# Operands of one decoder layer placed at multiples of 512 bytes in SBUF

## The reference, cut to what matters

```
h = rms_norm(x, ln1_g);  proj = h @ w_in                 # input projection
o = concat(gated_deltanet(proj...), sparse_attention(proj...))
x = x + o @ w_out                                        # output projection
h = rms_norm(x, ln2_g);  q = h @ w_query                 # 8 heads, two halves of 128
# per token and head: 16 best keys of 128 in each half, 16 best pairs -> gates, experts
act = gelu(h . u[expert]);  x = x + sum(gate * act * v[expert])   # 16384 experts
out = rms_norm(x, final_g)
```

## Time and profile before

| | |
|---|---|
| median of three runs | 1706.88 us |
| the profiled execution's own time | 1708.15 us |
| its span, first to last instruction | 1706.2 us |
| mean granted clock of TensorE, share of 2.4 GHz | 0.979 |
| TensorE busy with matmuls | 1630.3 us, 96% |
| VectorE, ScalarE, GpSimd busy | 78%, 40%, 32% |
| HBM traffic | 404 MB, 237 GB/s over the span |

### The profile page before, as it was taken

One profiled execution on the slowest core, in us unless ns is written; L12 is line 12 of the kernel. 1 busy time (PEld: TensorE's weight loads), 2 busy tenths in 40 slices (PEclk: granted clock), 3 DMA queues, 4 the chain that ended last, 5 costly groups with the idle time before them and its releaser, 6 DMA issues.

```text
span 1706.2 us, 26801 instructions
## 1 busy us (share of the span) xinstructions
PE 1630.3 (96%) x9303; PEld 1387.8 (81%) x9303; DVE 1333.9 (78%) x2453; ACT 682.1 (40%) x1070; POOL 540.2 (32%) x383
## 2 busy tenths in 40 slices
PE   7998888968999999999999999999999999999998
PEld 5876675545777999999999999998888788888886
DVE  6744568777642689999999999858888888888887
ACT  5574323154422343433354444433333333333334
POOL 2000000014420467888732334313333333322220
PEclk9999998879999999999999999999999999999999
DMA  4320010001223468888889999999999999999995
GB/s 140 99 95 27 2 39 1 25 25 50 87 86 125 143 196 289 282 286 280 262 295 359 336 348 342 340 335 401 371 372 376 368 372 367 379 353 334 350 354 191
DMA packets 148992, 404.47 MB, mean 237 GB/s; under 512 B 14084, under 2 KB 71684, under 8 KB 145448
## 3 DMA queue, kind: packets, MB, share of 16 engines
q1 hardware_dynamic: 108584, 243.92, 42.3%
q0 software_dynamic: 36864, 134.23, 20.7%
q10 hardware_dynamic: 3456, 25.17, 3.7%
HBM read 350.83 MB, written 52.44 MB: 236 GB/s over the span
## 4 chain that ended last, share of the span: by engine, by line
PE 54%; DVE 10%; DMA 1%; issue 1%; ACT 1%; POOL 0%; DVEq 0%; SPq 0%; ACTq 0%
PE bank L1555 10%; PE bank L1556 10%; PE bank L1557 10%; PE bank L2073 7%; PE bank L2077 7%; PE bank L2074 7%; DVE own_waste L1858 3%; PE bank L2097 3%; DMA front<-active_scratch 1%; DVE back L1909 1%; DVE rt_num L1880 1%; DVE rt_num L1873 1%; DVE rt_work L1874 1%; DVE rt_pos L1902 0%; DVE rt_pos L1899 0%
## 5 line engine op out<-in xcount | busy, mean ns | idle before, releaser
L2073 PE MATMUL bank<-hi_parts,rt_u_parts 128*128 128x384 f32 x1024 | 351.3, 343 | 0.0
L2074 PE MATMUL bank<-lo_parts,rt_u_parts 128*128 128x384 f32 x1024 | 344.1, 336 | 0.0
L1555 PE MATMUL bank<-rt_u_parts,rt_w_hi 128*128 128x512 f32 x768 | 304.1, 396 | 1.1 <-DVE rt_w_lo L1471 1.1
L1557 PE MATMUL bank<-rt_u_parts,rt_w_hi 128*128 128x512 f32 x768 | 303.7, 395 | 0.0
L1556 PE MATMUL bank<-rt_u_parts,rt_w_lo 128*128 128x512 f32 x768 | 303.7, 395 | 0.0
L1415 ACT ACTIVATE rt_u_parts<-raw 128x1024 fp32r<-128x1024 f32 x128 | 135.8, 1061 | 337.1 <-PE bank L1557 326.7
L1773 ACT ACTIVATE rt_u_parts<-raw 128x1024 fp32r<-128x1024 f32 x126 | 133.8, 1062 | 337.3 <-PE bank L2077 299.3
L2132 POOL DMA_INDIRECT qy<-v_dram,own_experts x128 | 133.3, 1041 | 361.0 <-DVE qy L1489 355.0
L2126 POOL DMA_INDIRECT h<-u_rows_dram,own_experts x128 | 172.7, 1349 | 236.4 <-DVE own_waste L1858 222.4
L1471 DVE TENSOR_TENSOR rt_u_parts<-raw,rt_u_parts 128x1024 fp32r<-128x1024 f32 x128 | 156.7, 1224 | 83.0 <-ACT rt_u_parts L1415 77.7
L1820 POOL TENSOR_TENSOR rt_u_parts<-raw,rt_u_parts 128x1024 fp32r<-128x1024 f32 x66 | 162.8, 2467 | 129.5 <-ACT rt_u_parts L1773 128.0
(11 more groups left out here) (356 smaller groups left out, 2602.8 us busy)
## 6 DMA issues: line engine op xcount, KB each, us to landing
raw<-u_dram SPq DMA_DIRECT2D x128, 512.0 KB
raw<-v_dram SPq DMA_DIRECT2D x128, 512.0 KB
active_scratch<-rt_act SPq DMA_DIRECT2D x128, 192.0 KB
gates_scratch<-front ACTq DMA_DIRECT2D x12, 1024.0 KB
gates_scratch<-back ACTq DMA_DIRECT2D x12, 1024.0 KB, 7.9
front<-gates_scratch SPq DMA_DIRECT2D x8, 1536.0 KB
front<-active_scratch SPq DMA_DIRECT2D x64, 192.0 KB
back<-active_scratch SPq DMA_DIRECT2D x64, 192.0 KB
```

Of the source, the lines that this page charges most:

```text
L1555: mm(bank, w_hi[:, j, block], v_hi[:, j, cols], start=False, stop=False)
L1557: last = mm(bank, w_hi[:, j, block], v_lo[:, j, cols], start=False, stop=stop)
L2073: mm(bank, u_hi[:, j % 2, chunk[c]], hi[:, c, 0:TD], start=c == 0, stop=False)
L2074: mm(bank, u_hi[:, j % 2, chunk[c]], lo[:, c, 0:TD], start=False, stop=False)
```

## The change: offsets, and no instruction

Three paddings and one move of a declaration. `aligned` allots an unused tensor that fills up to the next multiple of 512. It is called ahead of `x_stream` and ahead of `conv`. `w`, `w_hi` and `w_lo` are declared first in the route stage instead of last but one. Each engine's instructions are the same, in the same order.

```diff
+LINE = 512
...
@@ route_stage
+        w, w_hi, w_lo = sb("w", [P, 2, TD]), sb("w_hi", [P, 2, TD], F32R), sb("w_lo", [P, 2, TD], F32R)
         act_s = sb("act", [P, 4, TD])
...
         iota, row_of = sb("iota", [P, PTOP], BF16), sb("row_of", [P, P], F16)
-        w, w_hi, w_lo = sb("w", [P, 2, TD]), sb("w_hi", [P, 2, TD], F32R), sb("w_lo", [P, 2, TD], F32R)
...
@@ build
+        def aligned(ctx, name, unit):
+
+            short = -nc.sbuf_base % unit
+            if short:
+                ctx.enter_context(nc.sbuf_tensor(name, [P, short // 4], F32))
+
+        aligned(outer, "stream_place", LINE)
         x = outer.enter_context(nc.sbuf_tensor("x_stream", [P, DC, T], F32))
...
+            aligned(inner, "conv_place", LINE)
             conv, conv_parts = twins(inner, "conv", QKV_T)
```

## The result

The changed kernel took 1688.46 us, the median of four runs (1684.09 to 1689.56), against 1708.87 us for the kernel before (four runs, 1706.8 to 1710.9). The ratio is 0.9876, with a 95% interval from 0.9852 to 0.99. The forecast was 1688 us.

What follows compares the result with a forecast made beforehand. It took TensorE's distance between matmul starts as the bound. Value stage 15.2, minus 1 for a stall, plus tail 4.3 gave 18.5 us off 1708.15: 1689.7 profiled, 1688 at the median, range 1678 to 1709.

Steps and rivals of the forecast that it cites:

- What bounds: Value stage and tail run at TensorE's pace; with the matmul count unchanged, only the distance between starts could shrink.
- The value stage, 15.2 us: Moving w_hi and w_lo from 416 to 0 takes 2304 matmuls from 233.3 to 226.7 ns each, saving 15.2 us.
- the one stall: Value stage before: VectorE waited 3.2 us for activations behind a load of gates, of which 1.1 reached TensorE.
- a further stall: Value stage: 1 us taken off the gain for one more place where transfers come late.
- The transfers rival: Value stage: gate loads stall TensorE more, losing some 9 us of the 15, so 1697 us; chance 0.08.
- The tail, 4.3 us: Moving conv from 480 to 0 takes 7.5 ns off each of the tail's 576 matmuls, 4.3 us.
- Everything else, 0: Input and route stages, operands going from 128 to 0, were taken to keep their distances: 0 us.
- the rival of a whole line: All stages: the 13.3 ns surplus comes from operands beginning inside a 512-byte unit; 71 us less, 1636; chance 0.07.
- The cause: Float32r matmuls: weights starting off a multiple of 64 (or 128) cost about 7 ns more per matmul.
- The rival of the slower side: Value stage: equal remainders make accesses meet, adding 5 ns on 2304 matmuls, +11.5 us, so 1718; chance 0.06.
- The rows on plain float32: Mixer stage: L1159 at 592 ns and L386 at 591 were read as not feeling the start; 0, bound 1 us.

Runs made afterwards that it cites:

- w_alone: Kernel before with only w, w_hi and w_lo moved, from remainder 416 to 128 (by 512); ratio 0.9897.
- conv_alone: Kernel before with only conv moved, from remainder 480 to 0, hi and lo staying at 128; ratio 0.9993.
- by32: Changed kernel with rt_u_parts, conv and w at remainder 32, hi, lo and qy left at 0; 1696.12 us, one run.
- moving32: Changed kernel with hi, lo, raw, front, qy and rt_u_parts at remainder 32, conv and w left at 0; 1705.20 us, one run.
- mapC: Changed kernel with rt_u_parts at remainder 128, conv at 448 and w at 320; 1698.73 us, one run.
- conv128: Kernel before with only conv moved, from remainder 480 to 128, w staying at 416; ratio 0.9981.
- both128: Kernel before with conv and w at remainder 128 and nothing else moved; ratio 0.9891, median 1688.99 us.
- mapA: Changed kernel with conv at remainder 256 and w at 128, all that moves at 0; 1704.37 us, one run.
- mapB: Changed kernel with conv at remainder 64 and w at 256, all that moves at 0; 1688.77 us, one run.
- w16: Changed kernel with w_hi and w_lo starting 16 bytes behind a multiple of 512, conv at 96; 1706.33 us, one run.
- cols_apart: Changed kernel with route matmuls at 512 columns, value stage at 384, rt_u_parts at 32, conv at 320, w at 0; 1829.10 us, one run.
- cols_equal: Changed kernel with route matmuls at 512 columns, value stage at 384, rt_u_parts, hi, lo and w at 0, conv at 192; 1806.21 us, one run.

## Why the prediction was right in time and wrong in cause

*What bounds.* Right. TensorE's distances were 19.5 of the 24.0 us between the two profiles, and nothing else was late next.

*The value stage, 15.2 us.* Right: the distance fell by the 6.6 ns that were taken, to a tenth of a nanosecond. w_alone shows it by itself, 0.0103 of 1709, 17.6 us, of which 1.5 may be the one stall. The 1 us that I took off for a further stall had the wrong sign: no stall came, and the one of before went as well (16.8 us by the profile). The transfers rival is refuted by 383 GB/s without a wait.

*The tail, 4.3 us.* Right for the change, 4.2 in the profile. As a term of its own it would have been wrong: I priced `conv` from 480 to 0, which alone gives (234.3 − 232.8) × 576 = 0.9 us. It comes only because `hi` and `lo` go to 0 as well, which the prediction did not count as needed. That the change did both is luck for this term.

*Everything else, 0.* Right. The input stage stayed at 389 ns and the route stage at 173.3, so the rival of a whole line is out: with all at 0, the 13.3 ns are there as before.

*The cause.* This step failed: "All three are multiples of 32. Only 128 is a multiple of 64 or of 128." From stages that all have the moving operand at 128, I took the difference between 128 and 416 or 480 for a property of the weights' own start. The same rows allow another reading, that weights at 128 are good since what moves is at 128. The moving operand had one remainder in all rows, so they could not tell these apart, and the prediction should have said so and given the reading a chance. It did use it, to take the value of 226.7 ns "where weights and moving operand have one remainder", and that is why the number held. conv_alone (weights at 0, a multiple of 64, and still 232.8 ns), by32 and moving32 decide it: what counts is the weights' address less the moving operand's.

*The rival of the slower side* assumed the opposite of what is true: equal remainders are the good case.

*The rows on plain float32.* Each plain float32 matmul stands as two records in the trace: eight matmuls of L386 in the program, 16 records. So the 591 and 592 ns are of half a matmul, and there was one ahead of the L362 at 82.78, not two. That plain float32 does not feel placement at all is not so, though it came to nothing in the sum. In the changed kernel the weights of this matmul (L387 there; `cst`, at 128) and its moving operand (`h2`, at 0) are 128 apart, where both lay at 128 before:

```profile
L387 PE MATMUL bank<-h,cst x16: 590/593/667, 76.1 to 123.3; 128*128 128x512 f32 x16
```

The median record is 593 ns instead of 591, and after eight of the 16 records the next one starts 433 ns later instead of 428 or 429, some 0.04 us in all. It was not tested further. In moving32, with the two 96 apart, they are as before.

## What to carry to other kernels

For float32r matmuls that follow closely, look at the distance between starts, not at durations, and compare stages of one shape. (In mapC's value stage L1557 has a median duration of 388 ns, below the changed kernel's 389, though the stage's mean distance is 228.9 instead of 226.7.) If they differ, put weights and moving operand at addresses that are equal by 256 bytes; the absolute place did not matter in any run (both at 0, both at 32 and both at 128 gave 226.7 ns). When rows are compared, write down what is the same in all of them: that is what they can't speak for.

## What the runs showed of the hardware

At 512 columns, by the bytes that the weights are ahead of the moving operand:

| apart by 256 | apart by 512, and the run | ns |
|---|---|---|
| 0 | 0: changed kernel, w_alone, conv128, both128, by32; 256: mapA, mapB | 226.7 to 227.1 |
| 16 | 16: w16 | 233.3 |
| 32 | 32: by32; 288: kernel before, value stage | 233.2; 233.3 |
| 64 | 64: mapB; 320: cols_apart | 233.4; 233.3 |
| 96 | 96: w16; 352: kernel before, tail | 234.3; 234.3 |
| 128 | 128: mapA; 384: conv_alone | 232.4; 232.8 |
| 192 | 192: mapC, cols_equal; 448: mapC | 228.9, 229.0; 229.4 |
| 224 | 480: moving32, tail and value stage | 233.3; 233.3 |

These are of the tail and the value stage. Each pair that differs by 256 agrees within about half a nanosecond, across stages with another order of weights and other work beside them; 16 and 224 were met at one distance only. At 384 columns (route stage, third product) the equal case is 173.3, 32 apart 173.4, and 128 apart 175.7.

At full clock the best case has 13.3 ns more than one column per cycle of 2.4 GHz, at 384 as at 512 columns. Where the granted clock is 0.50, 1.2 GHz, 384 columns take 0.32 us from start to start, which is one column per cycle and nothing more. No run touched this surplus, and what it is remains open. So does the mechanism. A natural reading, not shown, is that the weights for the next matmul are read while the present one streams, and that the two reads meet or miss each other by their addresses; but in all these runs the next weights have the same remainder as the present ones, and no run tells them apart.

The Trainium skill says that TensorE has two SBUF read ports and that loading the next weights doesn't take read bandwidth from the running matmul (TensorE: Matmul & The Clock Gate, Step-by-step: what each phase is for). If the cost comes from that load, the rows here do not agree at 512 columns of float32r: the distance grows by up to 7.6 ns (226.7 to 234.3) with nothing changed but where the operands lie. No run shows that it is this load.
